# Experts of a decoder layer: gather for four at once, and a scatter of f32r high and low parts

## What is computed

```
logits = x2 @ w_router + b_router
top_v, top_i = top_k(logits, 4);  gate_w = softmax(top_v)
for each expert e and its tokens:
    hh = x @ w_gu[e] + b_gu[e]                      # 1024 -> 2048
    gate = min(hh[:, :1024], 7);  up = clip(hh[:, 1024:], -7, 7)
    act = (up + 1) * gate * sigmoid(1.702 * gate)
    y[token] += gate_w * (act @ w_down[e] + b_down[e])   # 1024 -> 1024
out = layer_norm(alpha * h + y)
```

## Time and profile before

| | |
|---|---|
| median of 3 runs | 1332.47 us (1332.32 to 1335.02) |
| span of the profiled execution | 1332.5 us (its own time is that of the median run) |
| TensorE busy | 1273.7 us, 96% |
| VectorE, ScalarE busy | 439.0 us (33%), 231.0 us (17%) |
| read from HBM | 447.43 MB, 341 GB/s over the span |
| mean granted clock of TensorE | 0.987 |
| expert loop | from about 353 us; last weights' matmuls end at 1308 us |

### The profile page before, as it was taken

One profiled execution on the slowest core, in us unless ns is written; L12 is line 12 of the kernel. 1 busy time (PEld: TensorE's weight loads), 2 busy tenths in 40 slices (PEclk: granted clock), 3 DMA queues, 4 the chain that ended last, 5 costly groups with the idle time before them and its releaser, 6 DMA issues.

```text
span 1332.5 us, 17082 instructions
## 1 busy us (share of the span) xinstructions
PE 1273.7 (96%) x6538; PEld 704.5 (53%) x6538; DVE 439.0 (33%) x877; ACT 231.0 (17%) x364; POOL 30.3 (2%) x45
## 2 busy tenths in 40 slices
PE   6999999999899999999999999999999999999993
PEld 5999999988534434343443434343443434343431
DVE  3465556644331331313131231313131231313135
ACT  4353334320111011010101011010101011011112
POOL 1000000100000000000000000000000000000002
PEclk9999999999889999999999999999999999999997
DMA  9644536693589999999999999999999999999981
GB/s 310 214 127 131 166 100 182 204 385 119 181 331 381 416 417 416 417 418 417 418 417 416 416 416 418 417 418 417 418 417 417 417 416 417 418 417 417 417 338 40
DMA packets 110266, 454.19 MB, mean 341 GB/s; under 512 B 8551, under 2 KB 39441, under 8 KB 77420
## 3 DMA queue, kind: packets, MB, share of 16 engines
q1 hardware_dynamic: 106084, 439.35, 82.9%
q0 software_dynamic: 4144, 14.30, 3.3%
HBM read 447.43 MB, written 6.31 MB: 341 GB/s over the span
## 4 chain that ended last, share of the span: by engine, by line
PE 91%; DVE 4%; issue 2%; DMA 1%; SPq 1%; ACT 1%; DVEq 0%; ACTq 0%
PE bank L953 33%; PE bank L976 17%; PE bank L667 13%; PE bank L932 10%; PE bank L997 4%; PE bank L751 3%; PE bank L726 2%; PE bank L962 1%; DMA ring<-in_w_in 1%; PE bank L965 1%; PE bank L808 1%; DVE arena L1657 1%; DVE arena L1644 1%; PE bank L891 1%; PE bank L940 1%
## 5 line engine op out<-in xcount | busy, mean ns | idle before, releaser
L953 PE MATMUL bank<-ring,arena 128*64 128x512 f32 x1536 | 349.9, 596 | 0.0
L953 PEld LDWEIGHTS bank<-ring,arena 128*64 128x64 f32 x1536 | 119.5, 137 | 206.2 <-issue 206.2
L667 PE MATMUL bank<-arena_r,ring_r 128*128 128x320 f32 x848 | 184.4, 318 | 3.5 <-DVE ring_r L1308 3.5
L976 PE MATMUL bank<-ring,arena 128*64 128x512 f32 x768 | 169.3, 593 | 1.3 <-ACT arena L1246 1.3
L1635 DVE TENSOR_TENSOR arena<-bank,arena 128x512 f32<-128x512 f32 x64 | 41.2, 686 | 359.5 <-PE bank L965 359.5
L667 PEld LDWEIGHTS bank<-arena_r,ring_r 128*128 128x128 f32 x848 | 140.0, 190 | 5.7 <-DVE ring_r L1308 3.7
L1628 DVE COPY arena<-bank 128x512 f32<-128x512 f32 x32 | 22.1, 691 | 328.1 <-PE bank L953 328.0
L932 PE MATMUL bank<-arena 128*128 128x128 f32 x720 | 127.9, 308 | 0.0
L953 PE MATMUL bank<-arena 128*64 128x512 f32 x512 | 119.4, 593 | 1.5 <-ACT arena L1228 1.5
L997 PE MATMUL bank<-arena 128*128 128x512 f32 (+1 forms) x192 | 93.0, 613 | 21.7 <-DVE arena L1657 15.8
L932 PEld LDWEIGHTS bank<-arena 128*128 128x128 f32 x720 | 97.9, 188 | 28.1
(11 more groups left out here) (223 smaller groups left out, 902.5 us busy)
## 6 DMA issues: line engine op xcount, KB each, us to landing
ring<-in_w_gu SPq DMA_DIRECT2D x192, 1024.0 KB, 14.9
ring<-in_w_down SPq DMA_DIRECT2D x96, 1024.0 KB, 17.7
arena<-in_w_gu SPq DMA_DIRECT2D x64, 1024.0 KB, 13.0
arena<-in_w_down SPq DMA_DIRECT2D x32, 1024.0 KB, 16.4
ring<-in_w_in SPq DMA_DIRECT2D x22, 1024.0 KB, 6.4
arena<-in_state_gla POOLq DMA_DIRECT2D x4, 1024.0 KB, 8.9
out<-arena POOLq DMA_DIRECT2D x4, 1024.0 KB, 5.2
ring<-in_w_branch_gla SPq DMA_DIRECT2D x4, 1024.0 KB, 5.9
```

The costliest lines, as they stand in the source:

```text
L667: last = mm(o[:, 0:NT], w[a][:, c, f0:f0 + 128], rhs[b][:, c, :], start=c == 0 and a + b == 0, stop=c == chunks - 1 and a == 1)
L953: last = mm(ex[i][side * CAP:(side + 1) * CAP, :], xgt[:, j, half * CAP:(half + 1) * CAP], w[:, i * D + side * 512:i * D + (side + 1) * 51 ...
L976: last = mm(ex[4][side * CAP:(side + 1) * CAP, :], actt[:, 2 * j + c, :], w[:, c, side * 512:(side + 1) * 512], start=j == 0 and c == 0, s ...
```

## The change

The units of work become groups of four experts. `onehot` now holds two pairs; VectorE makes all four experts' one-hots with three operations (`make_four`). `gather_four` brings 256 columns per matmul, 12 matmuls ahead of a down phase and 12 behind it. The first group is still gathered in two halves of one pair each, the second after the first down phase. `onehot_w` is gone: `turn_slots` transposes the plain one-hot, and three matmuls of 32 columns with `gw` give each slot its gate weight (`slot_w`). ScalarE scales the expert's output by it and writes it as f32r, the high part. VectorE's new `low_output` computes the same product again, minus the high part, as the low part. The scatter multiplies the f32r one-hots with both parts into the same bank. `ln2` moves to a place that is in the ring until the last expert, and its two loads wait for the first unit of that expert's up phase (`LN2_FREE`). Buffers are laid out anew. In diff form, cut to the core:

```diff
-            def gather(pair_count):
-                pe.wait_ge(onehot_ready, pair_count)
+            def gather_four(half):
+                for c in range(4):
+                    f0 = (4 * half + c) * 128
+                    for t, (t0, n) in enumerate(TILES):
+                        last = mm(ex[6 + c // 2][:, (c % 2) * 256:(c % 2 + 1) * 256], hrow[0:n, t, f0:f0 + 128],
+                                  onehot[0:n, :, t, :], start=t == 0, stop=t == 2)
+                last.then_inc(gathered, 1)
+            def turn_slots(pair):
                 for t, (t0, n) in enumerate(TILES):
-                    last = nc.tensor.transpose(ex[5][:, t0:t0 + n], onehot_w[0:n, t, :], ident[0:n, 0:n])
+                    nc.tensor.transpose(ex[5 + pair][:, t0:t0 + n], onehot[0:n, pair, t, :], ident[0:n, 0:n])
+                for t, (t0, n) in enumerate(TILES):
+                    last = mm(ex[5 + pair][:, NT:NT + NE], onehot[0:n, pair, t, :], gw[0:n, t, :], start=t == 0, stop=t == 2)
                 last.then_inc(slots_turned, 1)
@@ scatter
-                    mm(ex[5 + i % 3][0:n, :], slot_t[:, t0:t0 + n], res[:, half * 512:(half + 1) * 512],
-                       start=True, stop=True).then_inc(pieces, 1)
+                    for a in range(2):
+                        last = mm(ex[5 + i % 3][:, :], slot_t[:, of_quad, t0:t0 + 128],
+                                  res_parts[a][:, half * 512:(half + 1) * 512], start=a == 0, stop=a == 1)
+                    last.then_inc(pieces, 1)
@@ TensorE, first pair of a group (first: the group of experts 0 to 3)
+                turn_up(e)
+                if not first:
+                    pe.wait_ge(added, quad * 12 - 6)
+                    scatter(quad * 2 - 1, 1, e, quad)
+                expert_up(units(True, 4 * q + 1, m), 1)
+                ...
+                turn_slots(0)
+                turn_slots(1)
+                expert_down(e, units(False, 4 * q, m))
+                if first:
+                    pe.wait_ge(slot_ready, 1)
+                    gather_pair(1)
+                turn_up(e + 1)
+                if first:
+                    pe.wait_ge(xgt_ready, 2)
+                expert_up(units(True, 4 * q + 2, m), 2)
+                pe.wait_ge(res_ready, e + 1)
+                expert_down(e + 1, units(False, 4 * q + 1, m))
@@ second pair
+                turn_up(e)
+                scatter(quad * 2, 0, e, quad + 1)
+                expert_up(units(True, 4 * q + 3, m), 3)
+                if last:
+                    pe.wait_ge(act_ready, e + 1)
+                    turn_up(e + 1)
+                    expert_down(e, units(False, 4 * q + 2, m))
+                else:
+                    ...
+                    gather_four(0)
+                    expert_down(e, units(False, 4 * q + 2, m))
+                    pe.wait_ge(xgt_ready, quad * 2 + 3)
+                    gather_four(1)
+                    turn_up(e + 1)
+                    expert_up(units(True, 4 * q + 4, m), 0, rest=quad * 2 + 4)
+                pe.wait_ge(res_ready, e + 1)
+                expert_down(e + 1, units(False, 4 * q + 3, m))
@@ ScalarE
-                    last = A(res[half * CAP:(half + 1) * CAP, side * 512:(side + 1) * 512],
-                             ex[4][side * CAP:(side + 1) * CAP, :], ACT.Copy)
-                last.then_inc(res_ready, 1)
+                    last = A(res_parts[0][p0:p0 + CAP, side * 512:(side + 1) * 512],
+                             ex[4][side * CAP:(side + 1) * CAP, :], ACT.Copy, scale=slot_w[p0:p0 + CAP, pair:pair + 1])
+                last.then_inc(res_high, 1)
@@ VectorE
+            def low_output(idx, pair, half):
+                dve.wait_ge(res_high, idx + 1)
+                ...
+                    last = V.scalar_tensor_tensor(res_parts[1][p0:p0 + CAP, f0:f0 + 512], ex[4][side * CAP:(side + 1) * CAP, :],
+                                                  slot_w[p0:p0 + CAP, pair:pair + 1], res_parts[0][p0:p0 + CAP, f0:f0 + 512],
+                                                  ALU.mult, ALU.subtract)
+                last.then_inc(res_ready, 1)
+            def quad_of_blocks(quad, first=False, last=False):
+                gated(e, e, e * 4)
+                if not first:
+                    add_pieces(quad * 2 - 1)
+                keep_up(e + 1)
+                low_output(e, 0, 0)
+                gated(e + 1, e + 1, e * 4 + 4)
+                keep_up(e + 2)
+                low_output(e + 1, 0, 1)
+                gated(e + 2, e + 2, e * 4 + 8)
+                add_pieces(quad * 2)
+                ...
@@ GpSimd's queue
+            pool.wait_ge(up_used, LN2_FREE)
             pool.dma_start(ln2[0], ln2_g[0:1, :].broadcast_to([128, D])).then_inc(ln2_in, 16)
```

More of the change, by code:

```diff
@@ L158 @@
 XGT = 6144
-OHW = 7168
-ACTT = 7552
-G1 = 8064
 OH = 8704
-U1 = 9088
-SG = 9600
-HG = 10112
-HU = 10624
-RES = 11136
+SLOT_T = 9472
+ACTT = 10112
+G1 = 10624
+U1 = 11136
+SG = 11648
 RK = 12352
@@ L891, in first_gather @@
                         last = mm(ex[6 + c // 4][:, (c % 4) * 128:(c % 4 + 1) * 128], hrow[0:n, t, c * 128:(c + 1) * 128],
-                                  onehot[0:n, t, :], start=first and t == tiles[0] and c % 4 == 0, stop=not first,
+                                  onehot[0:n, 0, t, :], start=first and t == tiles[0] and c % 4 == 0, stop=not first,
                                   skip_group_check=True)
@@ L1004, in pair_of_blocks @@
                 turn_up(e)
                 if not first:
-                    scatter(pair - 1, e)
-                expert_up(units(True, 2 * p + 1, m), 1)
-                turn_slots(pair + 1)
+                    pe.wait_ge(added, quad * 12 - 6)
+                    scatter(quad * 2 - 1, 1, e, quad)
+                expert_up(units(True, 4 * q + 1, m), 1)
+                if first:
+                    pe.wait_ge(onehot_ready, 2)
+                else:
+                    pe.wait_ge(added, quad * 12)
@@ L1045, in _ @@
             pe.wait_ge(yb_used, 6)
-            pair_of_blocks(0, first=True)
-            with pe.Fori(0, NE // PERIOD - 1) as loop:
+            first_pair(0, first=True)
+            second_pair(0)
+            with pe.Fori(0, NE // PERIOD - 2) as loop:
                 m = pe.snap(loop)
-                pair_of_blocks(1, m)
-                pair_of_blocks(2, m)
-            pair_of_blocks(NE // 2 - 1, last=True)
-            scatter(NE // 2 - 1, NE)
+                first_pair(1, m)
+                second_pair(1, m)
+            first_pair(NE // PERIOD - 1)
+            second_pair(NE // PERIOD - 1, last=True)
+            pe.wait_ge(added, 6 * (NE // 2 - 1))
+            scatter(NE // 2 - 1, 1, NE, NE // 4)
             pe.wait_ge(lists_ready, 1)
@@ L1268, in _ @@
                 A(sm[0:n, t, :], lg[0:n, t, 0:4], ACT.Exp).then_inc(soft4_ready, 1)
-            keep_gathered(1)
+            keep_pair(0, 1)
             keep_gate(0)
-            pair_of_blocks(0)
-            with act.Fori(1, NE // 2 - 1) as pair:
-                pair_of_blocks(act.snap(pair))
-            pair_of_blocks(NE // 2 - 1, last=True)
+            quad_of_blocks(0, first=True)
+            with act.Fori(1, NE // 4 - 1) as quad:
+                quad_of_blocks(act.snap(quad))
+            quad_of_blocks(NE // 4 - 1, last=True)
             act.wait_ge(lists_ready, 1)
@@ L1656, in add_pieces @@
                     part = y[0:n, t, half * 512:(half + 1) * 512]
-                    V.tensor_tensor(part, part, ex[5 + i % 3][0:n, :], ALU.add).then_inc(added, 1)
-            def pair_of_blocks(pair, first=False, last=False):
-                e = pair * 2
+                    V.tensor_tensor(part, part, ex[5 + i % 3][128 - n:, :], ALU.add).then_inc(added, 1)
+            def low_output(idx, pair, half):
+                dve.wait_ge(res_high, idx + 1)
+                p0 = half * CAP
+                for side in range(2):
+                    f0 = side * 512
+                    last = V.scalar_tensor_tensor(res_parts[1][p0:p0 + CAP, f0:f0 + 512], ex[4][side * CAP:(side + 1) * CAP, :],
+                                                  slot_w[p0:p0 + CAP, pair:pair + 1], res_parts[0][p0:p0 + CAP, f0:f0 + 512],
+                                                  ALU.mult, ALU.subtract)
+                last.then_inc(res_ready, 1)
@@ L1661, in pair_of_blocks, with quad_of_blocks @@
+            def quad_of_blocks(quad, first=False, last=False):
+                e = quad * 4
                 gated(e, e, e * 4)
                 if not first:
-                    add_pieces(pair - 1)
-                    dve.wait_ge(slots_turned, pair)
-                make_onehot_w(0, e, e)
-                make_onehot_w(1, e + 1, e + 1).then_inc(onehot_w_ready, 1)
-                if not last:
-                    dve.wait_ge(gathered, pair + 1)
-                    make_onehot(0, e + 2)
-                    make_onehot(1, e + 3).then_inc(onehot_ready, 1)
@@ new lines, in quad_of_blocks @@
+                if not last:
```

(25 more changed lines are left out.)

156 lines of the change are left out of this document (92 added, 64 removed).

## The result

The changed kernel takes 1363.1 us (median of 4 runs, 1361.4 to 1364.2) where the one before takes 1333.1: a ratio of 1.0224, 95% interval 1.0212 to 1.0237, so 30 us slower. The forecast was 1325.2, with 0.08 for slower.

The account below looks back on a forecast made before the run. TensorE paced the loop, with weight transfers about 1% slower and setting the end after the change. Transfers +4.2, slack -11.5, low part +1.4, scatter -1.4 made 7.3 us less than 1332.5: 1325.2 us, range 1318 to 1334.

Parts of the forecast that it names:

- What bounds the kernel now: Main loop: TensorE paces at 119.5 us per four experts, weight transfers need 120.9 at 417 GB/s, about 1% slower.
- the transfers speed up: Rival on the weight stream: transfers go faster when TensorE frees slots sooner, ending at 1315 us; chance 0.04.
- Gather: Gathers of four experts: 48 instructions of 256 columns take 10.6 us instead of 16.9, saving 6.3.
- The clock: Rival: TensorE's clock falls while waiting for weights; a 10 us spell costs 5 us; chance 0.09, of which slower 0.02.
- the forecast's period: TensorE's time per four experts in the loop: 116.3 us against 119.5 before.
- The transfers as the limit: End of the loop: last weights land at 1299.1, after TensorE's 1291, so TensorE waits for weights from about the sixth group.
- The first group: The first four experts lose 5.5 us in all, through a narrow second gather, added gathers and a longer scatter.
- the last experts: The last four experts lose one gather but wait longer for slots, scatter and low part: about -4 us.
- The step from there to the end: After the last weights land at 1299.1, the last quarter of the down phase takes 1.8 us, ending at 1301.0.
- The end, behind the last down phase: Copy 1.2, low part 1.4, first piece 0.8, then six adds at 0.645 us, ending at 1308.4; norm and stores unchanged.
- The scatter block as the bound: Rival: scatter blocks exceed 9.0 us, each us beyond costing 16 over the kernel; chance 0.13, of which slower 0.05.

Follow-up runs that it names:

- late: The changed kernel with both scatters moved behind the next up phase, and VectorE's adds behind that phase's copies; 1328.7 us, 0.9966 against the kernel before.
- late_pad: The changed kernel with scatters behind the next up phase and the gather's third tile filled to 128 rows with zeros; 1328.2 us, 0.9955 against the kernel before.
- pair_pad: The kernel before with scatters behind the next up phase and its per-pair gather's third tile filled to 128 rows; 1322.1 us, 0.9912 against the kernel before.
- fill_pad: The changed kernel with idle-time matmuls ahead of the scatter's waits and the gather's third tile filled to 128 rows; 1330.8 us, 0.9973 against the kernel before.
- pad: The changed kernel with the gather's third tile filled from 64 to 128 rows with zeros; 1338.1 us, 1.0042 against the kernel before.
- Fill: The changed kernel with 8 added f32 matmuls per scatter in TensorE's idle time, results overwritten; 1347.4 us, 1.0100 against the kernel before.
- no_low: The changed kernel with the low part neither computed nor multiplied in, only the high part scattered; 1333.3 us, 0.9998 against the kernel before.
- before_late: The kernel before with each scatter moved behind the up phase that followed it, nothing of the change; 1324.8 us, 0.9935 against the kernel before.
- early_up: The kernel before with late scatters, first one-hots behind the first gate, expert 1's up phase ahead of the b_down products; 1336.2 us, 1.0027.

## Why the prediction was wrong

**What bounds the kernel now:** right. The transfers' limit is 120.9 us per group at 417 GB/s: late, late_pad and pair_pad run into it, and where TensorE waits for weights their groups take 120.6 to 120.7 us from one up phase to the same one of the next group; fill_pad touches it only at its very end. No queue length moved the rate (rival "the transfers speed up" falls).

**Gather: the first step that failed.** "f32 matmuls of 256 columns ran at 3.54 / 16 = 0.221 us each: 10.6 us." That row is of equal tiles. The gather's own row stood beside it: 8.45 / 48 = 0.176 us for 128 columns, more than half of 0.221, so it had a part that doesn't shrink with the columns. I used that number only as a bound for the slots. Measured: 6.75 us for 24, that is 0.281; that is the change of row count, and pad took it away (5.38, 0.224). 2.9 us per group.

**The clock: the second, and as large.** The rival had a price, 5 us for a spell of 10, but I looked for its place only in waits for weights, late in the kernel, and gave it 0.02 for slower. Its places are one scatter block and the slot products, in nearly every group: in the block the change takes away the f32 products that kept TensorE busy and adds 1.5 us of VectorE's work for which it waits. "The matmuls get cheaper ... but they aren't what this block waits for" was right for the time of the block, 8.97 us at full clock against 9.0, and left out what cheaper matmuls do to the clock. Fill shows it by putting work back: −15.7 us. Spells of 6.8 + 3.4 us per group cost 2.9 us. Mending both steps gives the forecast's period back: fill_pad's group takes 116.9 us, 116.3 were forecast. Of the case that the prediction cites (the Trainium skill, TensorE: Matmul & The Clock Gate, HAM oscillation), the pattern of bursts and waits is what the trace shows, with waits of about 2 us for VectorE beside cheap products. Its waits are for transfers and longer than the burst ahead of them, and the loop has none such in any run: 48 waits of up to 0.6 us behind 1.94 us of matmuls in pair_pad left the clock at 1.00.

**The transfers as the limit: a step that never came to bear.** The sum needed TensorE alone at 1291; it came to 1335.2. Of the 44 us, six groups at 6.4 make 39. The first group lost 7.6 us (the sixth up phase starts at 507.87 against 500.27 before) where 5.5 were forecast, its gathers being dearer. About 3 are left for the last experts, which have the same two spells (a down phase of 8.71 us, a scatter at half clock). The first 10 of the 44 would have been hidden behind the transfers (1301.0 against 1291), so the span is 34 us over the forecast (1359.5 against 1325.2). In late, where TensorE does meet the transfers, their term holds: last landing 1298.9 against 1299.1. The step from there to the end doesn't hold as told. The last down phase ends at 1301.9 against 1301.0, but it started behind the 3.0 us wait for the low part and not behind its weights; in pair_pad it ends 4.9 us after the last landing (1296.0 against 1291.1), where the forecast had 1.9.

**The end, behind the last down phase:** right. The chain of the changed kernel:

```profile
1328.09 7.09 PE bank L992 x32
1335.17 3.08 issue
1338.25 0.72 PE bank L1014 x2
...
1342.26 0.26 DVE arena L1729
```

7.3 us from the last down phase to the last add, forecast 7.4, and 17.0 from there to the end, 16.8 before.

**The scatter block as the bound:** its measured length of 8.97 us at full clock gave this rival no cause to happen; one of the two blocks grew to 9.98, and that by the clock. Its price of 16 us per us is not confirmed. no_low's 29.8 us look like 16 times 1.9, but its group is 3.4 us shorter by three terms: the two blocks 4.9 less, the down phase behind the slots 1.7 less, the up phases 3.2 more. Seven groups make 24 us, the shorter end most of the rest.

**Open:** what separates a place where the clock falls from one where it doesn't (in the changed kernel one scatter block of a group has a spell and the other, with waits as long, has none; the clock falls at the slot products in late, and not in pair_pad, whose pairs turn three pieces at a time and have no products of 32 columns); why the spells in the pair order last 13.7 and 20.5 us, and why none came in the profiled runs with the padded gather.

## What to carry to other kernels

Making a matmul cheaper in a place where TensorE then waits can cost more than it saves: before trusting the sum, ask of every block what busy time TensorE keeps in it, and read the granted clock there; moving the waiting chain under a dense phase is the cure, idle-time matmuls the makeshift. Price an instruction by its own row first, and only then by a foreign one: what its row costs beyond the columns stays. And where two resources are within 1% of each other, changing the order of work (8.8 us here) or the shape of a tile (the last 3 us) can bring more than removing work.

## What the runs showed of the hardware

- In a gather of f32 matmuls of 256 columns, a change between tiles of 128 and 64 rows costs about 0.2 us beyond the 0.22 us per instruction; filling the tile up with zero rows is faster (5.38 us against 6.75 for 24 instructions).
- Eight matmuls per scatter that compute nothing of use took 15.7 us off 1363 (fill).
- A wait for weights of 0.2 to 1.8 us between eight dense matmuls left the clock at 1.00 (late, pair_pad), while waits of 1.6 to 2.7 us for VectorE between three or six f32r products brought it down in one of the two scatter blocks of a group of the changed kernel and in every block of no_low's loop.
- Spells of half clock of 13.7 us began in gathers of 128-column f32 matmuls behind a 0.8 us wait and three transposes (once in before_late's profiled run, twice in early_up's), and each cost 6.0 us.
- One core took in 417 GB/s for 400 us on end, with 14 or 21 us from issue to landing alike (before), and the same with TensorE waiting for weights (pair_pad).
